# Keys, cached keys and convolution ends turned on VectorE in blocks of 32 instead of on TensorE

## The reference, cut to what matters

```python
def _in_proj(h, w_in):
    p = h @ w_in                      # GLU a | GLU b | q | k | v | gates
    glu = p[..., :D_CONV] * jax.nn.sigmoid(p[..., D_CONV:OFF_Q])
    ...
def _stick_breaking(q, k, v, q_pos, k_pos):
    z = jnp.einsum('bqhd,bkhd->bhqk', q, k) * ATTN_SCALE
    log_1m = jnp.where(mask, jax.nn.log_sigmoid(-z), 0.0)
    tail = lax.cumsum(log_1m, axis=3, reverse=True) - log_1m
    a = jnp.where(mask, jnp.exp(jax.nn.log_sigmoid(z) + tail), 0.0)
    return jnp.einsum('bhqk,bkhd->bqhd', a, v)
# conv branch: causal depthwise convolution (31 taps) over glu, LayerNorm, swish, product
# merge: x += (sigmoid(gc) * conv + sigmoid(ga) * attn) @ w_out ; x += relu(rms(x) @ w_up)^2 @ w_down
# outputs: y, and per row the new keys, the new values, and the last 30 rows of the convolution's input
```

## Time and profile before

| | |
|---|---|
| median of 3 executions | 962.91 us (962.04 to 963.27) |
| profiled execution, its own time | 962.6 us |
| its span | 960.9 us |
| TensorE busy | 951.3 us, 99% |
| VectorE, ScalarE, GpSimd busy | 535.5, 529.4 and 257.1 us |
| granted TensorE clock | 0.998 of full speed |

### The profile page before, as it was taken

How to read it: one execution, slowest core, us unless ns; L and a number is a source line. 1 busy time by engine, 2 the same in 40 slices (tenths; PEclk the granted TensorE clock), 3 DMA queues, 4 the chain that set the end, 5 groups by cost and what they waited for, 6 DMA issues and landing times.

```text
span 960.9 us, 19501 instructions
## 1 busy us (share of the span) xinstructions
PE 951.3 (99%) x7569; PEld 933.2 (97%) x7569; DVE 535.5 (56%) x905; ACT 529.4 (55%) x826; POOL 257.1 (27%) x188
## 2 busy tenths in 40 slices
PE   8999999999999999999999999999999999999997
PEld 8999999999999999999999999999999999999997
DVE  6579898989898989897553332222111122221133
ACT  6787877878787868776833343333111133331143
POOL 5311010101010110101243434345334244443240
PEclk9999999999999999999999999999999999999999
DMA  6767566675747483759132333333323232333102
GB/s 179 172 148 156 134 141 157 126 172 112 186 98 179 103 195 94 164 137 218 46 111 88 87 88 89 87 88 110 90 88 88 64 88 87 87 111 97 55 23 94
DMA packets 165728, 111.35 MB, mean 116 GB/s; under 512 B 4638, under 2 KB 157486, under 8 KB 165691
## 3 DMA queue, kind: packets, MB, share of 16 engines
q1 hardware_dynamic: 147290, 77.72, 28.0%
q0 software_dynamic: 7632, 27.79, 16.1%
q10 hardware_dynamic: 10768, 5.32, 2.0%
HBM read 75.97 MB, written 7.06 MB: 86 GB/s over the span
## 4 chain that ended last, share of the span: by engine, by line
PE 97%; ACT 1%; DMA 1%; DVE 0%; issue 0%; ACTq 0%; DVEq 0%
PE dense L510 82%; PE z L622 3%; PE dense L815 3%; PE z L585 2%; PE z L656 2%; PE z L579 1%; PE dense L666 1%; PE z L510 1%; DMA w_lo<-w_raw 1%; ACT n L926 1%; PE z L589 1%; DMA x_tok<-in_x_prompt_dram 0%; PE z L807 0%; PE z L642 0%; PE z L661 0%; PE z L551 0%
## 5 line engine op out<-in xcount | busy, mean ns | idle before, releaser
L493 POOL TENSOR_TENSOR w_lo<-w_raw,w_hi 128x1024 fp32r<-128x1024 f32 x80 | 192.2, 2406 | 295.1 <-ACT w_hi L908 295.1
L510 PE MATMUL dense<-r_hi,w_hi 128*128 128x272 f32 (+1 forms) x1264 | 263.3, 291 | 1.3 <-DMA w_lo<-w_raw 0.7
L510 PE MATMUL dense<-r_lo,w_hi 128*128 128x272 f32 (+1 forms) x1264 | 263.0, 289 | 0.0
L510 PE MATMUL dense<-r_hi,w_lo 128*128 128x272 f32 (+1 forms) x1264 | 262.7, 289 | 0.0
L908 ACT ACTIVATE w_hi<-w_raw 128x1024 fp32r<-128x1024 f32 x134 | 140.7, 1052 | 113.5 <-PE dense L510 102.7
L510 PEld LDWEIGHTS dense<-r_hi,w_hi 128*128 128x128 f32 x1264 | 198.1, 188 | 1.7 <-DMA w_lo<-w_raw 0.8
L510 PEld LDWEIGHTS dense<-r_lo,w_hi 128*128 128x128 f32 x1264 | 198.9, 188 | 0.7 <-DVE r_lo L1329 0.6
L510 PEld LDWEIGHTS dense<-r_hi,w_lo 128*128 128x128 f32 x1264 | 199.5, 188 | 0.0
L1347 DVE SCALAR_TENSOR_TENSOR acc<-conv_in,cw_cur,acc 128x574 f32<-128x574 f32 x232 | 173.6, 810 | 0.7
L470 POOL DMA_DIRECT2D w_lo<-w_raw x53 | 45.1, 851 | 372.0 <-ACT w_lo L910 372.0
L510 PE MATMUL dense<-s_hi,w_hi 128*128 128x272 f32 x640 | 132.2, 288 | 0.0
(11 more groups left out here) (266 smaller groups left out, 1315.2 us busy)
## 6 DMA issues: line engine op xcount, KB each, us to landing
w_raw<-in_w_in_dram SPq DMA_DIRECT2D x54, 512.0 KB, 5.5
w_lo<-w_raw POOLq DMA_DIRECT2D x53, 512.0 KB, 4.8
w_raw<-in_w_up_dram SPq DMA_DIRECT2D x32, 512.0 KB, 4.0
w_raw<-in_w_down_dram SPq DMA_DIRECT2D x32, 512.0 KB, 3.6
w_raw<-in_w_pw_dram SPq DMA_DIRECT2D x8, 512.0 KB, 3.6
w_raw<-in_w_out_dram SPq DMA_DIRECT2D x8, 512.0 KB, 3.5
x_tok<-in_x_prompt_dram SPq DMA_DIRECT2D x4, 512.0 KB, 6.4
out_dram<-v_tok ACTq DMA_DIRECT2D x8, 256.0 KB, 4.9
```

What stands on the lines that cost most here:

```text
L493: pool.tensor_tensor(w_lo[:, n], w_raw[:, n], w_hi[:, n].bitcast(F32), ALU.subtract).then_inc(lo_post, 1)
L510: mm = nc.tensor.matmul(out[:, h, 0:half], w[:, wslot, k, :], m[:, k, c0 + h * half:c0 + (h + 1) * half], start=(k == 0 and n == 0), stop= ...
```

## The change

The keys are no longer turned by TensorE. VectorE turns the K unit's PSUM tile in blocks of 32 by 32 into `k_blk` (576 columns), the cached keys into `ckT` (256 columns) and the ends of the convolution's input into `glu_blk` (64 columns). VectorE's full copy of K into `kT` goes; two short ones keep the last tile, `k_end`. In block form a partition holds, for one token of 32, pieces of 32 channels, so rows go out and the cached keys come in as pieces of 128 bytes: for each turn 12 DMAs of keys, 8 of convolution ends and 8 of cached keys, all on SyncE's queue, in place of five on ScalarE's and one on SyncE's. The cached keys of a block arrive sorted so that one product scores both tiles of a head: `ckT[:, hh, :]` holds 64 rows of each tile, and the moving side is `q_end`, twice 32 columns with zeros in the other head's rows, for which ScalarE makes two small copies per turn. The K unit writes its PSUM slot 232 columns in, so that the meta rows end on a block. `keys_back`, `cache_keys`, `keys_kept` and `keys_out` go, and `cumulate` stands right behind the K unit.

```diff
     def scores(i, hh, first=False):
-                score(*S_CACHE0, ckT[:, 0:P], SEQ, OUTTOK)
-                score(*S_CACHE1, ckT[:, P:2 * P], SEQ, OUTTOK)
+                score_cache()
...
+                def score_cache():
+                    apart = S_CACHE1[1] - S_CACHE0[1]
+                    out = z[:, 2, S_CACHE1[1] + DEC - 2 * apart:S_CACHE1[1] + DEC].rearrange("p (a c) -> p a c", c=apart)[:, :, apart - DEC:apart]
+                    at, step = ((META, DEC), (0, META + DEC))[hh]
+                    q = q_end[:, hh, at:at + 2 * step].rearrange("p (a c) -> p a c", c=step)[:, :, 0:DEC]
+                    nc.tensor.matmul(out, ckT[:, hh, :], q, start=False, stop=False, skip_group_check=True)
...
# TensorE, turn
-                    pe.wait_ge(q_kept, i + 1)
-                    keys_back(prev, 0)
-                    cache_keys(i, dense[:, 0, 1, 2 * P:4 * P]).then_inc(tile_done, 1)
-                    cumulate(2 * i - 1)
-                    pe.wait_ge(ktok_kept, i)
+                    cumulate(2 * i - 1)
+                    pe.wait_ge(q_kept, i + 1)
                     unit(2, 0)
                     values(prev)
...
# VectorE, turn
-                dve.wait_ge(tile_done, tile(i, T_KC) + 1)
-                nc.vector.tensor_copy(cols2(kT[:, 0:TOK], HALF), psum2(1, HALF))
-                nc.vector.tensor_copy(kT[:, TOK:TOK + META], dense[:, 1, 0, 0:META]).then_inc(k_kept, 1)
+                if not first:
+                    dve.wait_ge(k_out, K_OUT * i)
+                    dve.wait_ge(z_scored, 6 * i)
+                nc.vector.transpose(k_blk[:], k_slot[:, K_BLOCKS:K_BLOCKS + SQ - META + TOK]).then_inc(k_turned, 1)
+                nc.vector.tensor_copy(k_end[:, TOK - SEQ:TOK - SEQ + META], k_slot[:, K_AT:K_AT + META])
+                nc.vector.tensor_copy(k_end[:, 0:TOK - SEQ], k_slot[:, K_AT + SEQ:K_AT + TOK]).then_inc(k_kept, 1)
+                dve.wait_ge(ck_loaded, 16 * 2 * len(QUARTERS) * (i + 1))
+                nc.vector.transpose(ckT[:], ck_blk[:]).then_inc(ck_turned, 1)
...
                 conv(i, CONV[0])
+                if not first:
+                    dve.wait_ge(glu_out, GLU_OUT * i)
+                apart = 2 * PAD + DEC - SQ
+                nc.vector.transpose(glu_blk[:], conv_in[:, CTX_S + DEC - 2 * apart:].rearrange("p (w c) -> p w c", c=apart)[:, :, apart - SQ:]).then_inc(glu_turned, 1)
                 attn_gate(i)
...
# ScalarE, turn
-                act.wait_ge(tile_done, tile(i, T_KC) + 1)
-                nc.scalar.activation(ckT[:], pv[:, 0:2 * P] if first else dense[:, 0, 1, 2 * P:4 * P], ACT.Copy).then_inc(ckT_kept, 1)
-                    keys_kept(prev, tile(i, T_KC) + 1, 0)
...
# SyncE
+            def key_rows_out(i):
+                sync.wait_ge(k_turned, i + 1)
+                n = bass.ds(i, 1)
+                for a, rows in enumerate(QUARTERS):
+                    fs = slice(a * SQ, (a + 1) * SQ)
+                    sync.dma_start(nkp[META:META + SEQ, n, fs].rearrange("(b i) n j -> i b (n j)", i=SQ), k_blk[rows, SQ:SQ + SEQ].rearrange("i (b j) -> i b j", j=SQ)).then_inc(k_out, 16)
+                    sync.dma_start(nkp[0:META, n, fs].rearrange("i n j -> i (n j)"), k_blk[rows.start + SQ - META:rows.stop, 0:SQ]).then_inc(k_out, 16)
+                    sync.dma_start(nks[:, n, fs].rearrange("i n j -> i (n j)"), k_blk[rows, SQ + SEQ:]).then_inc(k_out, 16)
...
             def loads(i, first):
                 for u in range(LOOP_UNITS):
...
-                    if u == 0:
-                        if not first:
-                            sync.wait_ge(ckT_kept, i)
-                        sync.dma_start(ck_tok[:], ...).then_inc(ck_loaded, 16)
+                    if u == 2:
+                        if not first:
+                            sync.wait_ge(ck_turned, i)
+                        for a, rows in enumerate(QUARTERS):
+                            for h in range(2):
+                                sync.dma_start(ck_blk[rows, h].rearrange("i (b j) -> i b j", j=SQ), ...).then_inc(ck_loaded, 16)
+                    if u == 4 and not first:
+                        glu_rows_out(i - 1)
                     if u == 5:
+                        key_rows_out(i)
                         if not first:
                             sync.wait_ge(pv_done, i)
                         sync.dma_start(cv_tok[:], ...).then_inc(cv_loaded, 16)
```

More of the change, by code:

```diff
@@ L42 @@
 N_GROUPS = (3 + 2 * ROUNDS) * GROUPS_PER_STAGE
-T_Q, T_K, T_KC, T_V, T_VT, T_A, T_B, T_G = range(8)
-LOOP_TILES = 8
+T_Q, T_K, T_V, T_VT, T_A, T_B, T_G = range(7)
+LOOP_TILES = 7
 X_TILES = 5
@@ L55 @@
 X_EMPTIED = (3, 2)
-FIRST_POST = X_TILES + KC * LOOP_TILES + 1
+FIRST_POST = X_TILES + KC * LOOP_TILES
 WARM_UP = 8
@@ L67 @@
 LAST, N_LAST = (1, 400), META + DEC
+SQ = 32
+K_AT = 512 - (META + SEQ + DEC) // 2
+K_BLOCKS = K_AT - (SQ - META)
 S_CACHE0, S_CACHE1, S_OWN = (2, 272), (2, 448), (1, 416)
@@ L142, in build @@
         HEAD_ROWS = (slice(0, HD), slice(HD, P))
+        QUARTERS = [slice(a * SQ, (a + 1) * SQ) for a in range(P // SQ)]
+        K_OUT, GLU_OUT = 16 * 3 * len(QUARTERS), 16 * 2 * len(QUARTERS)
         sq = n32[:].rearrange("p a c -> p (a c)")[:, 0:D]
@@ L173, in build @@
         vT = sb("vT", [P, KEYS], where=loop)
-        ck_tok = sb("ck_tok", [P, 2, P], where=loop)
+        ck_blk = sb("ck_blk", [P, 2, P], where=loop)
         start = ExitStack()
@@ L181, in build @@
         start.close()
-        q_end = sb("q_end", [P, 2, META + DEC], where=loop)
-        ckT = sb("ckT", [P, 2 * P], where=loop)
+        q_end = sb("q_end", [P, 2, 2 * (META + DEC)], where=loop)
+        END_AT, OTHER_AT = (0, DEC), (META + DEC, 0)
+        ckT = sb("ckT", [P, 2, P], where=loop)
         a_sb = sb("a_sb", [P, TOK], where=loop)
@@ L190, in build @@
         heads2 = (sp, ez)
-        kT = sb("kT", [P, KEYS], where=loop)
+        k_end = sb("k_end", [P, P], where=loop)
         v_tok = sb("v_tok", [P, 5, P], where=loop)
-        k_tok = sb("k_tok", [P, 5, P], where=loop)
-        glu_tok = sb("glu_tok", [92, P], where=loop)
+        k_blk = sb("k_blk", [P, SQ - META + TOK], where=loop)
+        glu_blk = sb("glu_blk", [P, 2, SQ], where=loop)
         cv_tok = sb("cv_tok", [P, 2, P], where=loop)
@@ L420, in _ @@
             sync.wait_ge(y_out, 16 * 7)
+            sync.wait_ge(k_out, K_OUT * KC)
+            sync.wait_ge(glu_out, GLU_OUT * KC)
         @block.gpsimd
@@ L575, in scores, with score_last @@
                     pe.wait_ge(q_doubled, i + 1)
-                def score(bank, off, keys, q0, q1):
-                    return nc.tensor.matmul(z[:, bank, off:off + q1 - q0], keys, q_end[:, hh, q0 - SEQ + META:q1 - SEQ + META], start=False, stop=False, skip_group_check=True)
+                def score_last():
+                    bank, off = LAST
+                    return nc.tensor.matmul(z[:, bank, off:off + N_LAST], k_end[:], q_end[:, hh, END_AT[hh]:END_AT[hh] + N_LAST], start=False, stop=False, skip_group_check=True)
+                def score_cache():
[4 more added lines that the diff above has]
+                    nc.tensor.matmul(out, ckT[:, hh, :], q, start=False, stop=False, skip_group_check=True)
                 def score_split(bank, off, j, q0):
@@ L613, in scores @@
                 score_split(bank, off, 1, q0)
-                score(*LAST, kT[:, 4 * P:5 * P], SEQ - META, OUTTOK).then_inc(z_scored, 1)
+                score_last().then_inc(z_scored, 1)
             def cumulate(head):
@@ L667, in turn_back @@
                 return mm
[L669 to L679, removed]
             def turn(i, prev=None):
@@ L713, in turn @@
                     pe.wait_ge(ga_log, i)
-                    unit(1, 1)
+                    unit(1, 1, out=keys2)
                 if first:
-                    cache_keys(i, pv).then_inc(tile_done, 1)
                     unit(2, None, out=z[:, 0:2])
@@ L1159, in _ @@
             high_post(1, 3)
-            act.wait_ge(kv_out, 16 * 8 * KC)
+            act.wait_ge(v_out, 16 * 3 * KC)
+            act.wait_ge(k_out, K_OUT * KC)
+            act.wait_ge(glu_out, GLU_OUT * KC)
             act.preload_act_table_set("silu_and_others")
```

72 lines of the change are left out of this document (35 added, 37 removed).

## The result

Thirteen executions of the changed kernel have a median of 964.84 us (963.58 to 966.42), against 962.91 us before. The ratio is 1.0022, with a 95% interval of 1.0014 to 1.0030: slower by 1.9 us. The profiled execution took 963.88 us, its span 962.1 us, against 962.6 and 960.9.

The account below looks back on a forecast made before the run. TensorE was taken as the bound, with VectorE's loop 0.5 us shorter taking over. Sum: -0.41 + 1.3 + 7 x 0.25 - 0.81 + 0.3 = +2.1 us, forecast 965.0 us; own range 961.5 to 967.5, wider range 961 to 972.

Parts of the forecast that it names:

- The second loop: VectorE's GLU product to gating, TensorE's mask to GLU b unit, then ScalarE: 49.43 us against a turn of 49.94.
- What left TensorE: Per turn, eight turned tiles (0.80 us) and two products with cached keys (0.20 each) saved: 1.20 us shorter on TensorE.
- What came to VectorE: Three turnings, less two copies gone, add 0.49 to 0.69 us per turn at a copy's pace; 0.70 taken.
- The bracket: VectorE's added time per turn if turning runs at a copy's pace: 0.49 to 0.69 us.
- the surcharge for turning: On VectorE, upper end of turning at twice a copy's time per column: 0.94 us more, 1.64 per turn.
- rival (b): VectorE's turning costs twice a copy's time per column: 6.6 us more, 971.6 us; chance 0.15.
- The turn: In the loop, 50.19 us, 0.25 more than 49.94; TensorE waits 1.45 us at bank 1's mask in seven turns.
- The first turn: Before the fourth unit: TensorE 0.41 us sooner, then 1.3 us waiting for the low half beside key rows.
- From the second turn on: Key rows' delay to the fourth unit's low half, up to 2.6 us, is hidden by 3.4 us in hand.
- Behind the loop: Six turned tiles and the second head's product go, -0.81 us; 0.3 of it lost to a low half's wait.
- Rival (a): VectorE has unseen slack, so TensorE's saving comes out in full: 9.6 us less, 953.3 us; chance 0.08.
- Rival (c): Key rows in 128-byte pieces are dear and hold up low halves in each turn: about 7 us, 972; chance 0.15.

## Why the prediction was right, and where it was not

The time was forecast at 965.0 and came at 964.84. The main mechanism was right. That the sum came so close is luck: one step of it was wrong, and errors of both signs made up for each other.

**The second loop.** Right: VectorE's stretch from the GLU product to the gating became the bound, TensorE waits at the mask of bank 1 in seven turns, 1.4 us on the mean where 1.45 was forecast. The three kernels with moved taps and the two with the product in halves show it.

**What left TensorE.** 1.20 us per turn were forecast, 1.40 measured (49.94 to 48.54, both with TensorE busy throughout). The turned tiles gave the 0.80. The product gave 0.23 per head and not 0.20 (0.42 against 0.19, from 136.92 to 137.11). Some 0.14 more I can't place. In the first turn the 0.20 for the two cached tiles was not gained: their place is idle instead, 0.33 us before the values unit (30.07), for a low half that GpSimd makes. The page's fall in busy time, 9.0 us, understates this: a record in front of a wait is counted up to its modelled end, so a turn with a wait of 1.3 us shows 48.76 us of work and one without shows 48.54.

**What came to VectorE.** 0.70 was taken, 0.58 measured. The turning of 576 columns lasts 0.78 us and takes 0.71 from start to start, where the copy's rate gave 0.68: a copy's pace. The 256 columns of the cached keys, from SBUF, take 0.37 from start to start, against 0.34 by the copy's rate. The bracket (0.49 to 0.69) held the 0.58, and the surcharge for turning was not there. So rival (b) is out. The Trainium skill ("VectorE: DVE Perf Modes", The three transpose paths) gives 311 ns for 128 by 128 in bf16; scaled by columns that was an estimated 1.40 us for 576, twice what the trace has.

**The turn.** 50.19 was forecast, 50.03 is the mean: +0.09 and not +0.25 per turn, mostly from the term above. Over seven turns this is 1.1 us less than in my sum.

**The first turn: the step that failed.** I forecast +0.9 net: TensorE 0.41 sooner and 1.3 us of waiting for unit 3's low half, because the key rows' traffic would slow that landing. There is no such wait. The first turn is late by 1.03 us, but by another way: 0.46 is the late start of this one execution, 0.22 was gained by the product, and 0.79 is the queue. SyncE's queue is held by twelve issues, the next turn's first weight load goes out 6.3 us later, and ScalarE, in program order, brings the lateness to the GLU product. I had asked which traffic runs beside the rows and that "they are over before the next wait of that queue"; I had not asked what else is queued behind them, and had taken 0.5 us for an issue where several took 1.0 to 1.4 us. The size agreed by chance. Rows issued behind the third load, and no rows at all, show that it is the queue and not the traffic: both have the 0.79 us back.

**From the second turn on.** The rows are hidden: right. But in the second turn too SyncE issued the next load 5 us late (92.96 against 87.92), with no one waiting for it; the margin was smaller than I said.

**Behind the loop.** -0.81 and +0.3 were forecast, -1.1 came. The DMA wait in front of the fourth gate unit stayed (0.58 us against 0.73) and took no part of the gain back; another 0.1 us or so I can't place.

**At the end.** Not forecast: +0.65 us through a load of instructions.

The profiled sum: +1.03 (first turn) + 0.65 (seven turns) - 1.1 + 0.65 = +1.2 us; I had +2.1, and the medians differ by 1.9. The smaller turn and tail made up for the end. The items explain the profiled pair only, and 0.46 of theirs is its late start; so about 1.1 us of what the medians differ by is not accounted for. It is of the size of the spread named above, and its cause stays open. The range was not quite what its terms give, either: 965.0 - 1.5 - 1.3 is 962.2, and not 961.5. **Rival (a)**, TensorE's saving in full, is what the kernel does as soon as three taps are moved: 953.1 against the 953.3 that I gave it. **Rival (c)**: pieces of 128 bytes do cost twice as much for a byte, but are not dear here. (They are 2,240 in a turn, not 2,304.) The Trainium skill ("DMA: Bandwidth & Descriptors", Specifications) names 512 bytes as the least for the full rate; by that rule the trace agrees in kind (15 ns for 128 bytes, 29 for 512), and the time does not depend on it.

## What to carry to other kernels

A page that says "TensorE 99%" tells where work can leave, not that the time will follow: look for the wait on another engine with the least margin, add up the loop through it, and compare it with what leaves. If that second loop takes over, look for work in it that may stand elsewhere: here three taps, moved by shifting four cuts of a table, turned +1.9 us into -9.5. When DMAs are added to a queue, list what stands behind them there, for the first turn by itself, before thinking of bandwidth; and where a loop has no slack, a lateness of the first turn is paid to the end.

## What the runs showed of the hardware

- VectorE turns fp32 in blocks of 32 at a copy's pace: 576 columns from PSUM 0.78 us (a copy of 560 takes 0.74), 256 columns from SBUF 0.45 us, 64 columns 0.24 us.
- Of the twelve issues of key rows of a turn on SyncE's queue most took 0.33 to 0.56 us, and some 1.0 to 1.5 us (five of twelve in the first turn, seven in the second, one in the third); the twelve for key rows took 9.9 us in the first turn, 12.3 in the second and 7.4 in the third.
- A load of instructions can delay data. In all eleven traces with one in the last microseconds the span ends 0.6 to 0.8 us later behind the last stores than in the three without. It moved by 13 us when sixteen instructions were added to ScalarE's program. The Trainium skill ("Runtime: NRT & Kernel Launch", Instruction fetch mechanics) calls the cost of such loads mostly hidden; this trace agrees in so far as only the last one shows a cost, of 0.6 to 0.8 us.
